# A hybrid decoder layer on one core: weight splits moved behind each slot's steps, deeper buffers for the last pair's output weights, an earlier load of the first pair's q

## The chip, the cores and the metric

One core of one Trainium2 chip. The metric is the device time of one execution in microseconds (us), median of several runs; lower is better. Short names: PE is TensorE, PEld its weight loads, DVE is VectorE, ACT is ScalarE, POOL is GpSimd, SP is SyncE, which here only issues DMAs.

## What is computed

One layer over 1024 tokens of width 2048, in float32 (the reference cut to what matters):

```
h = rms_norm(x); proj = h @ w_in                       # 2048 x 7448
A: 12 heads of 64, dilated causal windows (128,1),(512,4),(2048,16), QK norm, mixed by softmax denominators
B: 8 heads of 64, causal softmax attention with a forget bias c[t]-c[s], QK norm
C: 4 heads of gated linear attention (dk 96, dv 192), per-head RMS norm
mixed = concat(out_a * silu(az), out_b * silu(bz), out_c * silu(cz))
out = x + mixed @ w_out                                # 2048 x 2048
```

## The kernel before, in words

**Precision.** Each wide product is done as three matmuls on rounded halves: a float32 matrix is split into hi (ACT copies it, rounding) and lo (DVE subtracts hi from the raw values), and hi·hi, hi·lo and lo·hi are summed. The activations (act_hi, act_lo) are split once and stay in SBUF. The weights are streamed: a quarter is 128 x 512 numbers (256 KB); SP loads it into w_raw (2 places), ACT writes w_hi (`split_hi`, L827), DVE writes w_lo (`split_lo`, L1231), PE uses both. A split of a place waits until PE is done with the quarter that was there, and a load until the raw place has been split.

**Groups and slots.** The input projection goes in 58 groups of 128 columns. A group has four quarters, each used for two halves of the tokens, so 8 half quarters of 12 matmuls. Everything else is cut into steps and laid between them: a group has 8 slots, and in a slot PE does the slot's steps and then one half quarter (`group` of each engine, L877, L1234, L1708). In slots 0, 2, 4 and 6, ACT and DVE split the quarter after the next one and then do their steps of the slot. ACT evicts the results and stores them in DRAM (proj), from where the heads load them.

**GLA heads (C).** Four heads of three groups, 24 slots (`gla_steps`, numbers of slots at L77). Slot 1: gate. Slot 3: DVE's scan of the decay (L1373). From slot 6 on, seven levels, one per slot: DVE takes differences (L1384, L1385), ACT the exponential (L993), POOL makes q_level and k_level (L776, L779), two slots later PE multiplies them (L1782) and DVE puts the result under a mask (L1436). Slot 12 transposes v, slot 18 is the chain of seven states on DVE (L1410, L1413), slot 19 the silu of z (DVE L1421, then three wide activations on ACT), slot 20 the output (ACT L1023, L1029), slot 21 its norm on DVE (L1424), slot 23 the transposes on PE (L1827) and the final product.

**Attention pairs (A and B).** Ten pairs of heads, 32 slots each. A pair has 16 items (head, block of 128 queries); an item's score (L1874), mask (L1514) and exponential (L1105), scaling (L1524), transposes (L1887), split of the transposed weights (pt_hi L1113, pt_lo L1530) and product with v (L1901) stand in fixed slots (`steps_of`, L109). Between them stand the norms of the next pair's q and k: ACT squares (L1062), DVE sq_lo (L1458), PE sums (L1847), ACT log and root, DVE the norm, and in slot 26 and slot 2 of the next pair the stacks: ACT q_st and k_hi (L1082, L1083), DVE a cast to the other half (L1473), POOL the low parts (L801, L804). For the first pair these stand in one group of their own before it (`first_steps_of`): squares in slots 1, 2, 4, 5.

**Last pair.** Its first 8 slots carry the last group of the projection; the other 24 carry early quarters of the output projection (45 quarters of w_out, three rounds over 3, 3 and 2 tiles of tokens), at the slots of EARLY_SLOT: nine quarters in five slots. Their sums with the residual (`early_sums`, L1627) go to DRAM as partial. The rows of mixed are loaded and split meanwhile (`mix_hi_part` L1205, `mix_lo_part` L1633, slots 4 to 13). Their landing, and that of the weights (L582), is ordered by SP's program, which is in order: mixed and weights interleaved, the load of the last gate behind quarter 6 and a wait for eleven mix_lo parts, the residuals behind quarter 7, partial stores and their reloads three quarters into a round. Then follow three groups of 16 output quarters over all 8 banks (`out_quarter`, L1967).

**What sets the order.** Each engine and SP's queue run their own program strictly in order; semaphores between them count finished work. A wait in one step holds up all that stands behind it on that engine.

```
def group(s, row, steps):            # ACT, before
    for slot in range(8):
        if slot % 2 == 0:
            split_hi(s, slot // 2 + 1)
        ...
        steps(slot)
```

Of the kernel before, what the change touches and what calls it, by code (L numbers as in the profile page):

```python
# [15 lines left out]
P = 128  # L16
SEQ = 1024
# [81 lines left out]
EARLY = len(ROUNDS) * (KT - 1)  # L99
EARLY_SLOT = [8 + (n * 5) // 9 for n in range(EARLY)]  # L100
# [73 lines left out]
def build(nc, x, norm_g, w_in, a_q_gain, a_k_gain, b_q_gain, b_k_gain, fox_bias,  # L174
# [11 lines left out]
    with ExitStack() as ctx:  # L186
# [65 lines left out]
        gla = ExitStack()  # L252
        level_mask = sb("level_mask", [P, LEVELS, HEAD], scope=gla)
# [9 lines left out]
        ranks = ExitStack()  # L263
        rank_rows = sb("rank_rows", [GATE_ROWS, SEQ], F32R, scope=ranks)
        ranks.close()
        v_rows = sb("v_rows", [P, NT, C_DV], scope=gla)
        k_rows = sb("k_rows", [P, NT, C_DK], scope=gla)
        state = sb("state", [C_DK, NT, C_DV], scope=gla)
# [9 lines left out]

        pairs = ExitStack()
# [29 lines left out]

        def mix_row(k):  # L310

            return vz[:] if k in (LAST - 1, LAST) else act_lo[:, k, :].bitcast(F32)

# [55 lines left out]
        w_in_sem = [sem("w_landed0"), sem("w_landed1")]  # L369
        x_in = [sem(f"x_landed{b}") for b in range(X_BUFS)]  # L370
# [10 lines left out]
        def _(sp):  # L381
# [196 lines left out]
            def load_out_rows(n, kk, col):  # L578

                sp.wait_ge(lo_done, Q_OUT + n - 1)  # L580
                slot = (EARLY + kk) % 2 if not isinstance(n, int) else n % 2
# [12 lines left out]
            load_k(0, 0, A_WIDTH, 0)  # L594
# [57 lines left out]
            for n in range(2, EARLY):  # L652
                load_out_rows(n, n % (KT - 1), 0)
# [164 lines left out]
        def _(act):  # L818
# [20 lines left out]
            def split_hi_out(cg, kk):  # L839

                slot = (EARLY + kk) % 2
# [8 lines left out]
                act.wait_ge(w_in_sem[slot], 16 * (2 * (GROUPS + AHEAD) + (KT // 2) * (cg - 1) + (EARLY + kk) // 2 + 1))  # L850
                act.activation(w_hi[:, slot, :], w_raw[:, slot, :], ACT.Copy).then_inc(hi_done, 1)  # L851

            def split_hi_early(n):

                r, kk = (n - 2) // (KT - 1), (n - 2) % (KT - 1)
# [1165 lines left out]
```

## Time and profile before

| | us |
|---|---|
| median of 3 runs | 2213.92 |
| lowest, highest | 2213.67, 2214.6 |
| the profiled execution | 2212.89 |
| its span, first to last instruction | 2211.1 |
| mean granted clock of PE, share of full speed | 0.991 |

The profile is of one execution. Its views used below: the page (busy time of each engine, its share of the span, number of instructions); waits (engine and line, the engine and line it waited for, us in total, times, longest); windows (start and end, length, busy us and instructions of each engine, PEclk as share of full speed, DMA share, GB/s); timelines (start us, duration us, engine, line, operation, output<-inputs, shape, count, and in brackets the idle time before it and what ended it).

### The profile page before, as it was taken

What the parts mean: (1) busy time and instruction counts of PE and PEld (TensorE: products, weight loads), DVE (VectorE), ACT (ScalarE), POOL (GpSimd) and SP (SyncE); (2) the same over time, 40 slices, a digit from 0 to 9 for tenths busy, and PEclk for the clock granted to TensorE, in tenths of its full rate; (3) what the DMA queues carried; (4) which work ended last, traced back from release to release, by engine and by line L of the source; (5) the groups of instructions that cost most, each with busy time, mean ns of one, the idle gap of its engine ahead of it and who ended that gap; (6) DMA issues with size and microseconds to landing.
All of it is one profiled execution on the core that took longest, in us unless ns stands there. A gap on an engine that the chain in (4) does not pass through costs nothing.

```text
span 2211.1 us, 30018 instructions
## 1 busy us (share of the span) xinstructions
PE 2141.1 (97%) x11016; PEld 1815.6 (82%) x11016; DVE 972.3 (44%) x1611; ACT 865.4 (39%) x1466; POOL 239.9 (11%) x141
## 2 busy tenths in 40 slices
PE   6999999999989999999999999999999989899999
PEld 5788888888878888888888888888888867778887
DVE  6611436445434545444444445444444455522122
ACT  7311343434444444454444444454444454311110
POOL 0000324142320000001010000001010000000000
PEclk9999999999999999999999999999999999999999
DMA  6323323333132222222222222322222253323134
GB/s 217 78 67 86 94 69 91 102 76 104 49 103 70 63 76 72 85 67 66 72 71 81 71 70 76 94 81 79 64 90 81 84 207 118 119 100 106 69 126 143
DMA packets 189772, 201.16 MB, mean 91 GB/s; under 512 B 15992, under 2 KB 138920, under 8 KB 188544
## 3 DMA queue, kind: packets, MB, share of 16 engines
q1 hardware_dynamic: 172976, 169.70, 26.2%
q10 hardware_dynamic: 16720, 30.45, 3.7%
q8 instruction: 47, 0.77, 0.1%
q14 instruction: 29, 0.24, 0.0%
HBM read 151.33 MB, written 48.78 MB: 91 GB/s over the span
## 4 chain that ended last, share of the span: by engine, by line
PE 86%; DVE 4%; ACT 3%; issue 3%; DMA 3%; POOL 1%; ACTq 0%; SPq 0%; DVEq 0%; POOLq 0%
PE acc L1694 18%; PE acc L1696 18%; PE acc L1695 18%; PE turned L1887 3%; PE pv L1902 3%; PE pv L1901 3%; PE scores L1877 2%; DMA w_raw<-in_w_out_dram 2%; PE scores L1874 2%; PE pv L1782 1%; PE acc L1984 1%; PE turned L1984 1%; PE scores L1984 1%; PE turned L1985 1%; PE scores L1985 1%
## 5 line engine op out<-in xcount | busy, mean ns | idle before, releaser
L1694 PE MATMUL acc<-act_hi,w_hi 128*128 128x512 f32 x1856 | 740.9, 399 | 7.0 <-DVE w_lo L1231 2.4
L1696 PE MATMUL acc<-act_hi,w_lo 128*128 128x512 f32 x1856 | 727.4, 392 | 0.0
L1695 PE MATMUL acc<-act_lo,w_hi 128*128 128x512 f32 x1856 | 725.9, 391 | 0.0
L1231 DVE TENSOR_TENSOR w_lo<-w_raw,w_hi 128x512 fp32r<-128x512 f32 x224 | 182.3, 814 | 578.8 <-ACT w_hi L827 578.5
L1694 PEld LDWEIGHTS acc<-act_hi,w_hi 128*128 128x128 f32 x1856 | 350.8, 189 | 78.2 <-DVE w_lo L1231 5.0
L1696 PEld LDWEIGHTS acc<-act_hi,w_lo 128*128 128x128 f32 x1856 | 350.0, 189 | 76.8
L1695 PEld LDWEIGHTS acc<-act_lo,w_hi 128*128 128x128 f32 x1856 | 350.9, 189 | 67.1
L827 ACT ACTIVATE w_hi<-w_raw 128x512 fp32r<-128x512 f32 x224 | 140.8, 628 | 294.8 <-PE acc L1696 249.6
L1105 ACT ACTIVATE prob<-prob,neg_max 128x128 f32<-128x128 f32 (+7 forms) x160 | 124.5, 778 | 274.1 <-DVE neg_max L1514 274.1
L1530 DVE TENSOR_TENSOR pt_lo<-turned,pt_hi 128x128 fp32r<-128x128 f32 (+7 forms) x160 | 121.0, 756 | 160.6 <-ACT pt_hi L1113 159.7
L801 POOL TENSOR_TENSOR q_st<-raw,q_st 64x1024 fp32r<-64x1024 f32 x20 | 55.8, 2788 | 1053.2 <-ACT q_st L1082 1053.2
L1902 PE MATMUL pv<-pt_lo,v_st 128*128 128x128 f32 x720 | 169.1, 274 | 0.0
L1901 PE MATMUL pv<-pt_hi,v_st 128*128 128x128 f32 x720 | 160.8, 264 | 0.9 <-DVE pt_lo L1530 0.9
L1113 ACT ACTIVATE pt_hi<-turned 128x128 fp32r<-128x128 f32 (+7 forms) x160 | 103.5, 647 | 130.6 <-PE turned L1887 128.3
L1901 PEld LDWEIGHTS pv<-pt_hi,v_st 128*128 128x128 f32 x720 | 137.7, 191 | 7.6 <-DVE pt_lo L1530 1.3
L1902 PEld LDWEIGHTS pv<-pt_lo,v_st 128*128 128x128 f32 x720 | 137.7, 191 | 6.0
L1658 DVE TENSOR_TENSOR w_lo<-w_raw,w_hi 128x512 fp32r<-128x512 f32 x48 | 33.3, 693 | 213.3 <-ACT w_hi L851 213.3
L869 ACT ACTIVATE stage<-acc 128x512 f32<-128x512 f32 x112 | 66.8, 597 | 149.2 <-PE acc L1696 149.1
L851 ACT ACTIVATE w_hi<-w_raw 128x512 fp32r<-128x512 f32 x49 | 31.0, 632 | 229.1 <-PE side L1986 215.0
L1514 DVE CUSTOM_DVE_ANT_0 prob<-scores,logit_bias 128x128 f32<-128x128 f32 (+7 forms) x160 | 120.0, 750 | 0.5
L1887 PE MATMUL turned<-ident,prob 128*128 128x128 f32 x720 | 108.7, 278 | 2.5 <-DVE prob L1524 2.5
L1874 PE MATMUL scores<-k_hi,q_st 128*128 128x512 f32 (+1 forms) x240 | 90.4, 377 | 2.0 <-issue 1.2
(273 smaller groups left out, 2777.7 us busy)
## 6 DMA issues: line engine op xcount, KB each, us to landing
w_raw<-in_w_in_dram SPq DMA_DIRECT2D x240, 256.0 KB, 2.9
proj_scratch<-stage ACTq DMA_DIRECT2D x116, 256.0 KB, 2.1
w_raw<-in_w_out_dram SPq DMA_DIRECT2D x94, 256.0 KB, 3.1
raw<-proj_scratch SPq DMA_DIRECT2D x20, 512.0 KB, 3.5
act_lo<-mixed_scratch SPq DMA_DIRECT2D x7, 1024.0 KB, 5.1
res<-in_x_dram SPq DMA_DIRECT2D x24, 256.0 KB, 5.6
out_dram<-res SPq DMA_DIRECT2D x24, 256.0 KB, 3.1
sq<-proj_scratch SPq DMA_DIRECT2D x10, 512.0 KB, 3.4
```

The source lines that it names most:

```text
L827: act.activation(w_hi[:, slot, :], w_raw[:, slot, :], ACT.Copy).then_inc(hi_done, 1)
L1105: act.activation(prob[:, j % 2, 0:n], prob[:, j % 2, 0:n], ACT.Exp, scale=-1.0, bias=neg_max[:, j:j + 1], accum_out=denom[:, j:j + 1]).the ...
L1231: dve.tensor_tensor(w_lo[:, slot, :], w_raw[:, slot, :], w_hi[:, slot, :].bitcast(F32), ALU.subtract)\
L1514: dve.tensor_tensor_reduce(out=prob[:, j % 2, 0:n], in0=scores[:, 0:n], in1=bias, scale=1.0, scalar=3e38, op0=ALU.add, op1=ALU.min, accum_ ...
L1530: dve.tensor_tensor(pt_lo[:, 0:n], turned[:, 0:n], pt_hi[:, 0:n].bitcast(F32), ALU.subtract)\
L1694: pe.matmul(acc, hi, xh, start=first, stop=False)
L1695: pe.matmul(acc, hi, xl, start=False, stop=False)
L1696: mm = pe.matmul(acc, lo, xh, start=False, stop=end)
L1874: pe.matmul(scores[:, c0:c1], q, k_hi[:, h, c0:c1], start=True, stop=False)
L1887: mm = pe.transpose(turned[:, at], prob[:, j % 2, at], ident[:])
L1901: pe.matmul(o, v_st[:, h, t, :], pt_hi[:, at], start=(t == 0), stop=False)
L1902: mm = pe.matmul(o, v_st[:, h, t, :], pt_lo[:, at], start=False, stop=(t == i))
```

## The change

1. In `group` of ACT and DVE the split of a quarter comes behind the slot's steps; in the GLA heads slot 20 (G_OUT) keeps it ahead. In the last group of the projection the fourth split is that of early quarter 0, and early quarter 1 is split behind the group.
2. Early quarters get four places to land (two new ones, extra_raw, beside w_raw) and three for splits (extra_hi, extra_lo); they are split two ahead, behind the steps of the slot, and the sums of a round come ahead of the slot's steps. The new places lie in the memory of raw, so SP waits for the last pair's stacks before the first load, and the first four are loaded before mixed rows 4 to 6.
3. The output stage starts with tiles 2 to 7, then 0 and 1, each waiting only for the sums that its bank needs. Quarter and place are counted from the stage's start.
4. q of the first pair is loaded at the end of the last GLA head, once all level matmuls are done and the older group with its columns is stored, ahead of two weight quarters and of the head's store; k before the wait for that store. For this the GLA tiles are laid out anew: k_level lies where raw will, q_level where sq will.

```
+        k_level = sb("k_level", [C_DK, 2, SEQ], scope=gla)
+        q_level = sb("q_level", [C_DK, 2, HALF], scope=gla)
+        g_b = sb("g_b", [C_DK, SEQ], scope=gla)
...
+        v_rows = sb("v_rows", [P, NT, C_DV], scope=gla)
+        k_rows = sb("k_rows", [P, NT, C_DK], scope=gla)
+        state = sb("state", [C_DK, NT, C_DV], scope=gla)
         level_mask = sb("level_mask", [P, LEVELS, HEAD], scope=gla)
...
         g_z = sb("g_z", [C_DK, 2, SEQ], scope=gla)
-        g_b = sb("g_b", [C_DK, SEQ], scope=gla)
         g_t = sb("g_t", [C_DK, 2, SEQ], scope=gla)
-        q_level = sb("q_level", [C_DK, 2, HALF], scope=gla)
-        k_level = sb("k_level", [C_DK, 2, SEQ], scope=gla)
...
+        extra_raw = sb("extra_raw", [P, 2, HALF], scope=extra)
+        extra_hi = sb("extra_hi", [P, HALF], F32R, scope=extra)
+        extra_lo = sb("extra_lo", [P, HALF], F32R, scope=extra)
...
+        early_raws = [extra_raw[:, 0, :], w_raw[:, 0, :], extra_raw[:, 1, :], w_raw[:, 1, :]]
+        early_his = [w_hi[:, 0, :], extra_hi[:], w_hi[:, 1, :]]
+        early_los = [w_lo[:, 0, :], extra_lo[:], w_lo[:, 1, :]]
...
 def saved_of(pair, g):
     if first_pair(pair):
-        saved(S_FIRST_V if g == 2 else S_FIRST_V - 1)
+        saved(S_FIRST_V - (HEAD_GROUPS + 1, 1, 0)[g])
...
+def load_early_rows(n):
+    if n >= EARLY_RAWS:
+        sp.wait_ge(lo_done, Q_OUT + n - EARLY_RAWS + 1)
+    elif n % 2 == 1:
+        sp.wait_ge(lo_done, Q_OUT + n // 2 - 1)
+    sp.dma_start(early_raws[n % EARLY_RAWS], w_out_k[:, OUT_ORDER[n % (KT - 1)], 0:HALF])\
+        .then_inc(early_landed(n)[0], 16)
...
+sp.wait_ge(gla_lv, LEVELS * C_HEADS)
+load_q(0, 0, 0)
 for kq in range(2):
     load_quarter(S_FIRST_V, kq, 2 * A_WIDTH)
 store_head(C_HEADS - 1)
-load_q(0, 0, 0)
-
+load_k(0, 0, A_WIDTH, 0)
 sp.wait_ge(gla_saved, 16 * C_HEADS)
-load_k(0, 0, A_WIDTH, 0)
...
 load_mixed(0)
 load_mixed(1)
-load_out_rows(0, 0, 0)
+for split in (ql_done, qh_done, kh_done, k_other_done, kl_done):
+    sp.wait_ge(split, 2 * PAIRS)
+load_early_rows(0)
+load_early_rows(1)
 load_mixed(2)
 load_mixed(3)
-load_out_rows(1, 1, 0)
+load_early_rows(2)
+load_early_rows(3)
 load_mixed(4)
...
-def group(s, row, steps):
+def group(s, row, steps, first=None, split_after=None):
     for slot in range(8):
-        if slot % 2 == 0:
+        if slot == first:
             split_hi(s, slot // 2 + 1)
         if slot == 7:
             evac(s, 0)
         steps(slot)
+        if slot % 2 == 0 and slot != first:
+            (split_after or split_hi)(s, slot // 2 + 1)
     evac(s, 1)
     save(s, row)
...
+                group(S_LAST_Z, COL_B + 3 * B_WIDTH + (B_PAIRS - 1) * P, steps, split_after=split_last)
+                split_hi_early(1)
                 for slot in range(8, SLOTS + 1):
+                    steps(slot)
+                    for n in early_at(slot):
+                        split_next(n + 2)
...
+                for slot in range(8, SLOTS + 1):
+                    for n in early_at(slot):
+                        if n % (KT - 1) == 0 and n > 0:
+                            early_sums(n // (KT - 1) - 1)
+                    steps(slot)
+                    for n in early_at(slot):
+                        if n + 2 < EARLY:
+                            split_lo_early(n + 2)
+                        elif n + 2 == EARLY:
+                            split_lo_group(1, 0)
...
+                for t in (2, 3, 4, 5, 6, 7, 0, 1) if first else range(NT):
+                    if first and t == 6:
                         pe.wait_ge(o_summed, 4 * PAIRS)
-                        pe.wait_ge(partial_summed, NT)
+                    elif first and t in (7, 0, 1):
+                        pe.wait_ge(partial_summed, {7: ROUNDS[1][-1], 0: ROUNDS[2][0], 1: ROUNDS[2][1]}[t] + 1)
```

DVE's `group` changes in the same way as ACT's.

## Rows read from the trace of the kernel before

**Rows 1.** The page: busy us, share of the span and instructions.

```profile
PE 2141.1 (97%) x11016; PEld 1815.6 (82%) x11016; DVE 972.3 (44%) x1611; ACT 865.4 (39%) x1466; POOL 239.9 (11%) x141
```

**Rows 2.** Waits of PE over the span: us in total, times, longest.

```profile
PE acc L1944 <- DVE w_lo L1619: 17.5, 11, 3.6
...
PE side L1847 <- DVE sq_lo L1458: 8.8, 10, 4.9
PE pv L1782 <- POOL k_level L779: 6.1, 4, 1.6
...
PE turned L1887 <- DVE prob L1524: 2.5, 1, 2.5
PE acc L1984 <- DVE sq L1627: 2.5, 1, 2.5
...
PE acc L1944 <- DVE sq L1627: 0.8, 1, 0.8
```

**Rows 3.** Windows around and behind PE's gaps; the clock stands third from the end.

```profile
256.00:268.00 12.00, 10.44 (x56) 8.78 (x55) 9.37 (x9) 4.59 (x6) 9.50 (x6) 0.86 0.50 133
350.00:362.00 12.00, 10.52 (x63) 9.03 (x62) 9.90 (x10) 4.78 (x6) 8.34 (x6) 1.00 0.56 153
444.00:458.00 14.00, 12.45 (x58) 10.56 (x56) 9.92 (x10) 5.83 (x7) 9.75 (x6) 0.76 0.54 131
541.00:554.00 13.00, 11.44 (x60) 9.65 (x59) 10.43 (x10) 5.04 (x7) 8.93 (x6) 0.87 0.55 141
...
626.50:631.00 4.50, 4.50 (x13) 3.49 (x12) 1.39 (x2) 1.95 (x4) 0.00 (x0) 0.59 0.24 60
...
1790.00:1850.00 60.00, 47.49 (x220) 38.95 (x220) 36.66 (x51) 28.54 (x41) 0.00 (x0) 0.89 0.39 132
```

**Rows 4.** Timeline of the fourth GLA head, slot 6: weight subtract, first level.

```profile
539.69 0.69 DVE L1231 TENSOR_TENSOR w_lo<-w_raw,w_hi 128x512 fp32r<-128x512 f32 x1 [2.27 <-ACT w_hi L827]
540.30 0.68 DVE L1384 TENSOR_TENSOR g_t<-g_b 96x512 f32<-96x512 f32 x1
...
544.27 1.49 POOL L779 TENSOR_TENSOR k_level<-g_qk,g_t 96x512 f32<-96x512 f32 x1
```

**Rows 5.** Timeline at the end of the second and fourth GLA heads.

```profile
415.26 1.76 DVE L1424 TENSOR_TENSOR g_qk<-g_qk,o_rstd 128x1536 f32<-128x1536 f32 x1 [0.73 <-ACT o_rstd L1034]
...
417.45 1.04 PE L1827 MATMUL scores<-ident,g_qk 128*96 128x128 f32 x8
...
608.68 1.76 DVE L1424 TENSOR_TENSOR g_qk<-g_qk,o_rstd 128x1536 f32<-128x1536 f32 x1 [1.12 <-ACT o_rstd L1034]
...
610.58 1.05 PE L1827 MATMUL scores<-ident,g_qk 128*96 128x128 f32 x8
```

**Rows 6.** Timeline of ACT in the group before the first pair: its first square.

```profile
623.57 0.63 ACT L1062 ACTIVATE sq<-raw 128x512 f32<-128x512 f32 x1 [5.41 <-DMA raw<-proj_scratch]
```

**Rows 7.** Timeline of PE in the last pair: five of its eleven waits for w_lo.

```profile
1803.40 0.50 PE L1944 MATMUL acc<-w_hi,act_hi 128*128 128x512 f32 x1 [2.22 <-DVE w_lo L1619]
...
1841.93 0.79 PE L1944 MATMUL acc<-w_hi,act_hi 128*128 128x512 f32 x1 [2.31 <-DVE w_lo L1619]
...
1866.85 0.50 PE L1944 MATMUL acc<-w_hi,act_hi 128*128 128x512 f32 x1 [0.53 <-DVE w_lo L1619]
...
1907.24 0.50 PE L1944 MATMUL acc<-w_hi,act_hi 128*128 128x512 f32 x1 [1.29 <-DVE w_lo L1619]
...
1930.41 0.50 PE L1944 MATMUL acc<-w_hi,act_hi 128*128 128x512 f32 x1 [1.42 <-DVE w_lo L1619]
```

**Rows 8.** Timeline: a DVE operation beside one of POOL, in a head and in slot 26.

```profile
602.85 4.70 DVE L1231 TENSOR_TENSOR w_lo<-w_raw,w_hi 128x512 fp32r<-128x512 f32 x1 [6.39 <-ACT w_hi L827]
...
870.54 2.65 POOL L801 TENSOR_TENSOR q_st<-raw,q_st 64x1024 fp32r<-64x1024 f32 x1 [85.37 <-ACT q_st L1082]
871.00 2.75 DVE L1473 CAST k_hi<-raw 64x1024 fp32r<-64x1024 f32 x1
...
876.42 0.39 PE L1874 MATMUL scores<-k_hi,q_st 128*128 128x512 f32 x1
```

More of the change, by code:

```diff
@@ L99 @@
 EARLY = len(ROUNDS) * (KT - 1)
+EARLY_RAWS, EARLY_SPLITS = 4, 3
 EARLY_SLOT = [8 + (n * 5) // 9 for n in range(EARLY)]
@@ L651, in _ @@
             load_mixed(6)
-            for n in range(2, EARLY):
-                load_out_rows(n, n % (KT - 1), 0)
+            for n in range(4, EARLY):
+                load_early_rows(n)
                 if n == 6:
@@ L839, in split_hi_out @@
             def split_hi_out(cg, kk):
-                slot = (EARLY + kk) % 2
+                slot = kk % 2
                 if kk == 1:
@@ L1038, in gla_head @@
                 for g in range(HEAD_GROUPS):
-                    group(C_ALONE + HEAD_GROUPS * c + g, col[g], lambda slot: gla_steps(c, 8 * g + slot))
+                    group(C_ALONE + HEAD_GROUPS * c + g, col[g], lambda slot: gla_steps(c, 8 * g + slot),
+                          G_OUT - 8 * g)
             gla_head(0)
@@ L1174, in steps, with split_last @@
                             mix_hi_part(kk)
-                group(S_LAST_Z, COL_B + 3 * B_WIDTH + (B_PAIRS - 1) * P, steps)
-                for slot in range(8, SLOTS + 1):
-                    last_pair_slot(slot, lambda: steps(slot))
-            def last_pair_slot(slot, steps):
-                ahead = [n + 1 for n in early_at(slot)]
-                for n in ahead[:1]:
-                    split_next(n)
-                steps()
-                for n in ahead[1:]:
-                    split_next(n)
+                def split_last(s, kq):
+                    if kq < 4:
+                        split_hi(s, kq)
+                    else:
+                        split_hi_early(0)
+                group(S_LAST_Z, COL_B + 3 * B_WIDTH + (B_PAIRS - 1) * P, steps, split_after=split_last)
+                split_hi_early(1)
+                for slot in range(8, SLOTS + 1):
+                    steps(slot)
+                    for n in early_at(slot):
+                        split_next(n + 2)
             def split_next(n):
@@ L1232, in split_lo, with group @@
                     .then_inc(lo_done, 1)
-            def group(s, steps):
+            def group(s, steps, first=None, split_after=None):
                 for slot in range(8):
-                    if slot % 2 == 0:
+                    if slot == first:
                         split_lo(s, slot // 2 + 1)
                     steps(slot)
+                    if slot % 2 == 0 and slot != first:
+                        (split_after or split_lo)(s, slot // 2 + 1)
             def split_lo_half(n, kq):
@@ L1448, in gla_head @@
                 for g in range(HEAD_GROUPS):
-                    group(C_ALONE + HEAD_GROUPS * c + g, lambda slot: gla_steps(c, 8 * g + slot))
+                    group(C_ALONE + HEAD_GROUPS * c + g, lambda slot: gla_steps(c, 8 * g + slot), G_OUT - 8 * g)
             gla_head(0)
@@ L1652, in add_residual @@
                     dve.tensor_tensor(to, banks[t], to, ALU.add).then_inc(out_summed, 1)
-            def split_lo_group(cg, kk):
-                slot = (EARLY + kk) % 2
-                dve.wait_ge(hi_done, Q_OUT + EARLY + KT * (cg - 1) + kk + 1)
-                dve.tensor_tensor(w_lo[:, slot, :], w_raw[:, slot, :], w_hi[:, slot, :].bitcast(F32),
-                                  ALU.subtract).then_inc(lo_done, 1)
             for kk in range(KT):
@@ L1969, in out_quarter @@
                 at_end = kk == KT - 1
-                slot = EARLY % 2 if only else (EARLY + kk) % 2
+                slot = 0 if only else kk % 2
                 k = OUT_ORDER[kk]
@@ L1974, in out_quarter @@
                     pe.wait_ge(mix_lo, KT)
-                for t in range(NT):
-                    if kk == 0 and isinstance(cg, int):
+                first = kk == 0 and isinstance(cg, int)
+                for t in (2, 3, 4, 5, 6, 7, 0, 1) if first else range(NT):
+                    if first and t == 6:
                         pe.wait_ge(o_summed, 4 * PAIRS)
-                        pe.wait_ge(partial_summed, NT)
-                    elif kk == 0 or only:
+                    elif first and t in (7, 0, 1):
+                        pe.wait_ge(partial_summed, {7: ROUNDS[1][-1], 0: ROUNDS[2][0], 1: ROUNDS[2][1]}[t] + 1)
+                    elif not first and (kk == 0 or only):
                         pe.wait_ge(out_summed, NT * (cg - 2) + t + 1)
```

70 lines of the change are left out of this document (37 added, 33 removed).

## The prediction

> **What bounds the kernel now.** I read the page's shares first: TensorE is busy 97% of the span [rows 1], VectorE 44%. What the change can win is therefore TensorE's idle time, 70 us, and what a low clock costs after it. Next I asked for TensorE's waits, longest first in total [rows 2]. Four of those groups lie where the diff works: 17.5 us on the low parts of output weights (L1944), 8.8 us on sq_lo (L1847), 6.1 us on k_level (L1782), and 2.5 us each on prob (L1887) and on the partial sums (L1984). The waits of the start, before 110 us, are not touched. Then I read windows around the gaps for the granted clock [rows 3], and the timelines of all engines for what each gap hung on. The sum is made against the profiled execution, 2212.89 us with a span of 2211.1; the median shown, 2213.92, is 1.0 above it, and I add 1.0 at the end.
>
> **Split behind the steps, in general.** Nothing is added or removed here: one ScalarE copy and one VectorE subtract per weight quarter change places with the steps of their slot. TensorE needs the pair of them two half quarters later, and a half quarter of 12 matmuls takes some 2.7 us at full clock (4.5 us at clock 0.59 [rows 3]). So the split may be up to 5.4 us late, plus TensorE's own steps. In an attention slot the steps end with mask, exponential and perhaps a stack, some 4 us behind TensorE's score; the copy and subtract cost 0.6 to 0.7 each. I went through each even slot of the pair this way and found no deadline missed, with some 2.3 us left in the tightest, slot 26. The weight loads on SP wait for the subtract of two quarters before, so they go out later by the same 1 to 5 us, but are also wanted later; what stands behind them on SP (gate, values, next q and k) is released by stores that land later still. Cost 0, cover 2.3 us.
>
> **GLA levels, four heads.** TensorE's first level matmul (slot 8) waits 1.5 us for GpSimd's k_level, four times [rows 2]. The chain behind it: VectorE's slot 6 subtract of weights at 539.69, only then the decay differences at 540.30, an exponential, GpSimd until 545.76 [rows 4]. Before that subtract VectorE had stood idle 2.27 us for ScalarE's copy, which waits for TensorE. With the differences ahead of the subtract the chain starts 2.27 + 0.61 = 2.9 us earlier (the memset of slot 2, moved ahead of its subtract, adds a little), and the wait goes whole: 6.1. After three of the four waits the clock is low: 0.86 of 12 us, 0.76 of 14 and 0.87 of 13, which is 1.7, 3.4 and 1.7 lost; after one of them it stays at 1.00 [rows 3]. So the clock is worth 0 to 6.8 and I take 6.8, as the low stretch directly follows the gap each time. Gain 12.9.
>
> **End of a GLA head.** Here the new order costs. In slot 18 VectorE now subtracts weights after the seven state steps and before slot 19's maximum of g_z, on which ScalarE's chain (three wide activations, the output copies and squares) hangs. That chain ends in VectorE's normalisation, and TensorE's transposes wait for it: in the fourth head it ends at 610.44 and they start at 610.58. In the second head there are 0.43 us between [rows 5]. The chain is 0.6 later: 0.6 in two heads, 0.3 in the two with such slack. Loss 1.8, bounds 0 and 2.4.
>
> **First pair's q.** In the group before the first pair TensorE waits 4.9 us in one place [rows 2]: ScalarE's square had waited 5.4 us for the load of raw [rows 6], issued behind the store of the previous group. The diff waits for an older group and issues it in the last head, into memory that the level matmuls have left. Then squares and subtract end about 0.5 us before TensorE wants them. The 4.5 us after the gap ran at clock 0.59 [rows 3]: another 1.8. Of the 6.7, something comes back: k takes q's old place in the DMA queue, the third weight quarter lands behind it (before, too, ScalarE waited for it), and ScalarE, waiting for it in order, holds up the second log. I charge 0.5, bounds 0 and 3. The next wait, of the first score on GpSimd's stacks, hangs on TensorE's own sums and stays. Gain 6.2.
>
> **Nine pairs, slot 17.** The remaining nine waits on sq_lo make 8.8 − 4.9 = 3.9. Each is 0.4 to 0.5; mask, exponential and square stood behind the split in slot 16 (0.6 and 0.7), more than the wait. Gain 3.9.
>
> **Last pair.** Four landing places, three split places, and two quarters of lookahead. But both kernels split a slot's first quarter at the same point: behind the steps of the slot before. What goes is what hung on a second quarter, on landing or on a freed place: 0.5, 1.3 and 1.4 [rows 7], and the 2.5 of the partial sums, since the output stage now starts on four banks that hold none [rows 2]. What stays: 2.3 at 1841.93 [rows 7], behind an exponential, a mix copy and a mix subtract; the longest, 3.6 [rows 2], since the load of the eighth quarter still stands on SP behind the wait for mix_lo and the gate load; the 2.5 on prob, where the split moved from before to after and VectorE has as much ahead of it; some 0.8 for a round's sums, as now [rows 2]. At 1803.40 [rows 7] the landing is early now, but the steps of slot 8 (a gated product and a mix subtract of 1.2 each) hold the split: 2.2 becomes 0.9. The extra early loads stand in front of three mixed loads, which are not yet due. Gain 5.7 + 1.3 = 7.0; bounds: −3, if the loads delay the mixes, and the whole, below.
>
> **Sum.** 12.9 − 1.8 + 6.2 + 3.9 + 7.0 = 28.2. 2212.89 − 28.2 + 1.0 = 2185.7 us, 1.3% faster.
>
> **Rivals.**
> *Last pair nearly dense.* If the deeper places hide my remaining waits too, the last pair gives its 23.3 us of waits (17.5 + 2.5 + 2.5 + 0.8 [rows 2]) and 6.6 of slow clock (0.89 of 60 us [rows 3]), less 4.1 for sums and prob: 25.8 in place of 7.0, 2166.9 us. For it: TensorE's need per slot is above the others' busy time. Against: the chain of one slot is a latency, not a load.
> *Low clock stays.* If short matmuls in the GLA slots, not the gap, bring the clock down, levels give 6.1, the first group 4.4, the last pair 4: 6.1 − 1.8 + 4.4 + 3.9 + 4 = 16.6, 2197.3 us. For it: one 1.5 us gap without a fall.
> *The delay shows.* A new wait of 0.6 us on w_lo in each of the 50 groups from the first GLA head on would cancel it all, 2213 us. Against it the 2.3 us of cover.
> *A blocked subtract, slower.* Place: slot 26 of nine pairs. GpSimd's q low part starts at 870.54 and VectorE's cast after it takes 2.75; a weight subtract beside GpSimd's wide multiply of a head took 4.70 in place of 0.69 [rows 4, 8]. In the new order the cast should start at 869.8 and GpSimd at 870.0. If the cast loses, it ends at 873.2 and the weight subtract behind it waits for the next GpSimd op too, to 876; pt_lo and the mask follow, and TensorE's score at 876.42 [rows 8] comes 2.0 late. With 1.7 of slow clock each, 9 × 3.7 = 33 us: 2219 us. It decides from 28.2/9 = 3.1 us per pair. Against it: 0.2 us of lead, and a clock that need not fall. The Trainium skill (SBUF — State Buffer, Who interferes with whom) has a rule that speaks for this rival: a VectorE instruction with two SBUF inputs and a GpSimd one that reads SBUF shut each other out for a whole instruction, and the first to start wins. By that rule the weight subtract, now among the stacks, is always exposed and the cast's lead settles it; the 4.70 us row agrees.
>
> **How the numbers follow.** Forecast 0.53; low clock stays 0.22; last pair dense 0.12; delay shows 0.06; blocked subtract 0.07. Faster by over 0.2% (4.4 us, about what a measurement of this kernel can tell): 0.53 + 0.22 + 0.12 = 0.87; within it 0.06; slower 0.07. The range reaches 16 us beyond the forecast to the slow side, past the low-clock case, and 15 to the fast side, most of the way to the dense one: 2171 to 2202.
>
> **What would show it.** Right: no wait on k_level and clock 1.00 behind slot 8 of each head; TensorE's wait on g_qk (L1424's row) up to about 2 us in total; sq_lo waits under 1 us in total; no wait of the first output quarter on sums; 3 to 4 us still lost at the eighth early quarter. Wrong: waits on w_lo (L1231's row) above 3 us, casts of 2.75 followed by subtracts over 2 us in slot 26, or a score waiting for neg_max in every pair.

## The result, and the profile after

| | before | after |
|---|---|---|
| median, us | 2213.8 (4 runs) | 2177.01 (4 runs) |
| lowest, highest | 2212.33, 2214.6 | 2176.43, 2179.62 |
| the profiled execution | 2212.89 | 2176.6 |
| its span | 2211.1 | 2174.9 |

The ratio is 0.9837, with a 95% interval of 0.9825 to 0.9849: 36.8 us less. Forecast were 28.2 us less, 2185.7, with a range of 2171 to 2202. So direction and range held, and the gain was a quarter under-estimated. The question is which terms of the sum were short.

The page of the changed kernel, as for [rows 1]:

```profile
PE 2129.0 (98%) x11016; PEld 1807.6 (83%) x11016; DVE 1000.6 (46%) x1611; ACT 859.6 (40%) x1466; POOL 248.6 (11%) x141
```

TensorE has the same instructions and is busy 12.1 us less: some 9 of that is clock, an estimate from the mean granted clock of the two traces, 0.991 and 0.995. The rest of the gain is idle time. VectorE became 28 us busier with as many instructions, so some of its work is slower now. The page's group of its weight subtracts shows where, 207.6 us in place of 182.3:

```profile
L1266 DVE TENSOR_TENSOR w_lo<-w_raw,w_hi 128x512 fp32r<-128x512 f32 x223 | 207.6, 931 | 300.7 <-ACT w_hi L857 300.7
```

That costs nothing as long as nothing waits for it.

Waits of TensorE in the changed kernel, as in [rows 2] (total, times, longest, in us):

```profile
PE acc L1981 <- DVE w_lo L1656: 7.8, 6, 2.2
...
PE acc L1981 <- DVE extra_lo L1656: 3.1, 1, 3.1
PE acc L1731 <- DVE w_lo L1266: 3.0, 8, 1.4
PE turned L1924 <- DVE prob L1561: 2.5, 1, 2.5
...
PE acc L1981 <- DVE stage L1671: 0.5, 1, 0.5
PE scores L1864 <- DVE g_qk L1461: 0.2, 1, 0.2
```

The group on k_level is gone, and those on sq_lo and on the output sums; the 17.5 us on the early quarters' low parts are 7.8 + 3.1. The 2.5 us on prob are still there.

To see where the gain came from (36.7 us between the two traces up to the last matmul; the spans differ by 36.2), I took the first start of some TensorE instructions in both timelines and subtracted. The last column is what each stage gained.

```
stage, from the first start of ... to ...             before    after   gained
start of the program to head 1's gate matmul                              0.4
four heads, gate matmul to first level matmul                             6.8   (1.70, 1.66, 1.66, 1.76)
four heads, first level matmul to last transposes                         4.8   (1.35, -0.47, 2.78, 1.14)
last head's transposes to first pair's values         656.17   637.28     6.9
nine pairs                                                                6.0   (0.59 to 0.72 each)
last pair, values to first early quarter             1796.28  1769.35     2.1
first to last early quarter                          1935.95  1901.96     7.1
to the first output quarter                          1939.30  1902.65     2.7
output                                                                    0.1
```

(The columns give the time of the stage's end mark.) The clock behind slot 8 of a head, windows of the changed kernel at the places of [rows 3] (the granted clock third from the end):

```profile
256.00:268.00 12.00, 12.00 (x79) 10.82 (x78) 10.70 (x10) 4.30 (x5) 9.00 (x5) 1.00 0.46 132
...
442.00:456.00 14.00, 14.00 (x88) 12.21 (x86) 12.50 (x12) 5.13 (x7) 11.80 (x7) 1.00 0.41 112
535.00:548.00 13.00, 13.00 (x82) 11.35 (x81) 12.12 (x11) 4.56 (x7) 10.83 (x6) 1.00 0.44 121
```

TensorE is busy for every microsecond of them and keeps its upper level, where it had 0.86, 0.76 and 0.87. The last pair still has its gaps, in TensorE's timeline:

```profile
1776.02 0.50 PE L1981 MATMUL acc<-w_hi,act_hi 128*128 128x512 f32 x1 [0.74 <-DVE w_lo L1656]
...
1789.43 0.51 PE L1981 MATMUL acc<-w_hi,act_hi 128*128 128x512 f32 x1 [1.76 <-DVE w_lo L1656]
1796.23 0.50 PE L1981 MATMUL acc<-extra_hi,act_hi 128*128 128x512 f32 x1 [3.06 <-DVE extra_lo L1656]
...
1813.81 0.73 PE L1981 MATMUL acc<-w_hi,act_hi 128*128 128x512 f32 x1 [2.24 <-DVE w_lo L1656]
```

The first answers to the 2.22 at 1803.40 in [rows 7] (0.9 was forecast), the last to the 2.31 at 1841.93, the third to the 3.6 that was forecast to stay.

### The profile page after: what moved, and what is told of

The parts are those of the page before. It is cut to its first block, busy times and chain, and to the rows that moved or that the text cites. A ratio compares the mean times of both kernels' runs of the same rounds, so it can differ in the third digit from the quotient of the medians.

```text
span 2174.9 us, 30011 instructions
## 1 busy us (share of the span) xinstructions
PE 2129.0 (98%) x11016; PEld 1807.6 (83%) x11016; DVE 1000.6 (46%) x1611; ACT 859.6 (40%) x1466; POOL 248.6 (11%) x141
## 4 chain that ended last, share of the span: by engine, by line
PE 88%; DVE 5%; ACT 3%; DMA 2%; issue 2%; SPq 0%; ACTq 0%; DVEq 0%
PE acc L1731 18%; PE acc L1733 18%; PE acc L1732 18%; PE turned L1924 4%; PE pv L1939 4%; PE pv L1938 3%; PE scores L1914 2%; PE scores L1911 2%; PE pv L1819 1%; DMA w_raw<-in_w_in_dram 1%; PE side L1819 1%; PE turned L2023 1%; PE scores L2023 1%; PE acc L2023 1%; PE scores L2024 1%
## 5 line engine op out<-in xcount | busy, mean ns | idle before, releaser
L1266 DVE TENSOR_TENSOR w_lo<-w_raw,w_hi 128x512 fp32r<-128x512 f32 x223 | 207.6, 931 | 300.7 <-ACT w_hi L857 300.7
L1663 DVE TENSOR_TENSOR w_lo<-w_raw,w_hi 128x512 fp32r<-128x512 f32 x49 | 33.9, 693 | 214.5 <-ACT w_hi L881 214.5
```

Source lines behind the costliest of these rows:

```text
L1266: dve.tensor_tensor(w_lo[:, slot, :], w_raw[:, slot, :], w_hi[:, slot, :].bitcast(F32), ALU.subtract)\
```

## The experiments

Each kernel is the changed one with one edit, and each was timed in five rounds beside the kernel before. Where a difference is small, I go by the stage marks of its trace against those of the changed kernel, since medians of one kernel differ by a microsecond or two between sets of runs. One stage is too unsteady for that. From the first to the last early quarter the changed kernel took 132.6 us, and the traces of e1 to e5, e7, e9 and e10, which leave the order of that work alone, took 129.7 to 135.0. A difference there counts only if a named gap or an earlier mark stands outside the same nine traces.

**e1. One split back ahead, in the GLA heads.** (`first` takes a list of slots, on ScalarE and VectorE.)

```diff
-    group(C_ALONE + HEAD_GROUPS * c + g, ..., G_OUT - 8 * g)
+    group(C_ALONE + HEAD_GROUPS * c + g, ..., [G_OUT - 8 * g, G_LEVEL[0] - 8 * g])
```

> The changed kernel with one weight split, that of slot 6 of each GLA head, put back ahead of the slot's steps on ScalarE and VectorE. Theory: this split alone is what the k_level wait hung on, and the low clock behind it hangs on that gap: TensorE waits about 1.5 us on k_level in each of the four heads (6.1 in all), the clock falls behind at least three of them, and the time is 11 to 14 us above the changed kernel's 2177.0, that is 2188 to 2191. Rival, low clock from the short matmuls of those slots: the wait returns but nothing on top of it, +6 us, 2183. Rival, the whole group's splits matter and not this one: within 2 us of 2177.

Measured: 2191.88 us (2189.49 to 2193.51), ratio 0.9902 (0.9884 to 0.9921). Its wait on k_level, and the windows behind slot 8 of its four heads:

```profile
PE pv L1819 <- POOL k_level L809: 6.1, 4, 1.6
```

```profile
259.00:273.00 14.00, 13.85 (x85) 12.09 (x85) 12.90 (x10) 3.91 (x5) 9.73 (x8) 1.00 0.37 100
353.00:367.00 14.00, 13.73 (x70) 12.12 (x70) 12.53 (x9) 2.64 (x4) 9.38 (x7) 0.76 0.35 104
451.00:465.00 14.00, 14.00 (x80) 12.27 (x80) 12.66 (x11) 4.22 (x5) 9.93 (x7) 0.88 0.34 93
547.00:561.00 14.00, 14.00 (x79) 12.29 (x80) 12.76 (x10) 4.16 (x5) 9.92 (x7) 0.88 0.34 99
```

From the gate of head 1 to the end of head 4 it lost 13.1 us: 6.8 up to the level matmuls and 6.3 between them and the heads' ends. So one split decides the whole item. It also settles the rival on the clock: the same short matmuls run at 1.00 without the gap and at 0.76 and 0.88 with it, in three of four heads (before, it was another three: head 2 was spared there, head 1 here). A gap of 1.5 us costs 3.3 us a head on average: 2.0 in the head that was spared, 3.2 to 4.7 in the others.

**e2. One split back ahead, in the nine pairs.**

```diff
-    group(s0 + g, columns[g], lambda slot, g=g: steps_at(pair, 8 * g + slot))
+    group(s0 + g, columns[g], lambda slot, g=g: steps_at(pair, 8 * g + slot), [16 - 8 * g])
```

> The changed kernel with one weight split of each of the nine full pairs, that of slot 16, put back ahead of the steps on both engines. Theory: the nine waits on sq_lo hung on it alone. They come back at 0.4 to 0.5 us each, and since each pair became 0.59 to 0.72 shorter and not 0.43, the time is 5 to 7 us above 2177.0, 2182 to 2184. Rival: the pairs gained by the delay of all their splits together; then this one split gives back 0 to 2 us, 2177 to 2179.

Measured: 2184.63 us (2182.83 to 2185.48), ratio 0.9870 (0.9850 to 0.9891). Its waits of TensorE on sq_lo:

```profile
PE side L1884 <- DVE sq_lo L1495: 4.2, 10, 0.5
```

The pairs are 0.59 to 0.73 us longer each, 5.9 us in all, which is what the change had gained there. Nine waits of some 0.43 us stand for stages 0.66 us longer: the idle time in a row is less than what the stage loses. In the first pair, the last product's matmul and the sum behind it start at 693.16 and 693.84, 0.68 us apart; the same two start 0.11 apart in the changed kernel. That is 0.57 us lost, where the row has 0.41 in brackets.

**e3. The first pair's q loaded late.**

```diff
-            load_q(0, 0, 0)
             for kq in range(2):
                 load_quarter(S_FIRST_V, kq, 2 * A_WIDTH)
             store_head(C_HEADS - 1)
+            load_q(0, 0, 0)
             load_k(0, 0, A_WIDTH, 0)
```

> The changed kernel with the first pair's q loaded behind the store of the last head and behind two weight quarters, as before the change. Theory: the first group's gain of 6.9 us was this load alone: one wait of 4 to 5 us on g_qk (L1461's row) returns with low clock behind it, 2182.5 to 2184.5. Rival: the splits behind the steps gave part of it, as they let the first square start earlier; then at most 4 us return, below 2181.

Measured: 2180.90 us (2180.36 to 2182.52), ratio 0.9855 (0.9834 to 0.9876), which by the time alone is the rival's range, just below 2181. Up to the first pair's values it lost 4.3 us of the 6.9 gained: 3.1 up to the first sum and 1.2 behind it, where the clock was 0.89 from 616 to 620 us and 1.00 in the changed kernel. But this run undid only the load's place. The change did a second thing to it: it waits for the rows of an older group. ScalarE's first square, which in the kernel before had stood idle 5.4 us [rows 6]:

```profile
610.40 0.63 ACT L1097 ACTIVATE sq<-raw 128x512 f32<-128x512 f32 x1 [2.56 <-DMA raw<-proj_scratch]
```

It waits for the load here too, but only 2.6 us. The load was issued 0.5 us behind the head's store here (603.49, the store at 602.97), and 6.0 us behind it before (620.16, the store at 614.17). Counted from the last head's transposes, the square starts 11.0 us later here and 13.0 before. So the place is worth 4.3 us of the 6.9. The other 2.6 were not tried alone; the square's 2 us point to the group waited for. The load itself took longer here, 6.9 us to land beside the store and 3.4 before, so most of the earlier issue was not gained. The rival's reason, that the splits gave part of it, isn't needed: in both kernels the square waited last for the load. TensorE's wait is on sq_lo (2.9 us) and not on g_qk, as I had written in the expectation by a slip.

**e4. The output's first quarter in plain order.**

```diff
-                for t in (2, 3, 4, 5, 6, 7, 0, 1) if first else range(NT):
+                for t in range(NT):
```

(and both waits ahead of the first tile)

> The changed kernel with the first output quarter's eight row tiles in plain order, the waits for the output sums and the last partial sums all ahead of the first tile. Theory: 2.5 us of wait return there, 2179.5. Rival: the sums are done early enough now, since the last round's split no longer stands behind them; then under 0.5 us, 2177 to 2177.5.

Measured: 2180.51 us (2179.59 to 2182.94), ratio 0.9854 (0.9833 to 0.9875). The wait is back in TensorE's timeline:

```profile
1906.08 0.47 PE L2022 MATMUL acc<-w_hi,act_hi 128*128 128x512 f32 x1 [2.18 <-DVE sq L1671]
```

The last early matmul starts at 1903.05, 3.0 us ahead of this one; in the changed kernel it is 0.7. That part gives 2.3 us, as forecast.

**e5 and e9. The blocked subtract.** In the changed kernel VectorE's k cast in slot 26 starts 0.14 us before GpSimd's q low part and takes 0.69 us, in all nine pairs; before it had started behind it and taken 2.75 [rows 8]. So the race that the rival hung on was there, and the cast won it. (The twenty casts take 13.8 us in all, 32.3 before.) I delayed the cast:

```diff
                     elif name == "stack0" and next_kind is not None:
-                        stack(pair + 1, 0)
+                        [dve.memset(spare[:, 44 * i:44 * i + 44], 0.0) for i in range(3)]; stack(pair + 1, 0)
```

> The changed kernel with three small memsets (44 columns each, some 0.3 us together) ahead of VectorE's k cast in slot 26 of each of nine pairs, so that the cast starts after GpSimd's q low part instead of 0.14 us before it. The rival of the prediction, blocked subtract: the cast takes about 2.75 us, the weight subtract behind it is late or waits for GpSimd's next multiply, TensorE's next score or weight quarter comes late by 2 us, with low clock 3.7: up to 33 us above 2177.0, 2210. My theory: the cast does lose and takes 2.75, but the cover of 2.3 us takes most of it; 0 to 0.7 us per pair, 2177 to 2183. If the cast still takes 0.69, the race was not lost and nothing is said on it.

Measured: 2176.82 us (2175.89 to 2179.33), ratio 0.9838 (0.9820 to 0.9856). GpSimd and VectorE in slot 26 of the third pair:

```profile
851.09 2.91 POOL L831 TENSOR_TENSOR q_st<-raw,q_st 64x1024 fp32r<-64x1024 f32 x1 [85.61 <-ACT q_st L1117]
```

```profile
850.87 0.20 DVE L1609 MEMSET spare<- 128x44 f32 x3
851.08 0.69 DVE L1510 CAST k_hi<-raw 64x1024 fp32r<-64x1024 f32 x1
```

The three memsets took 0.20 us together, too little: the cast was at most 0.01 us ahead in all nine pairs, and that was enough. Nothing is said on the rival. So again, with a longer delay:

```diff
-                        [dve.memset(spare[:, 44 * i:44 * i + 44], 0.0) for i in range(3)]; stack(pair + 1, 0)
+                        [dve.reciprocal(spare[:, i:i + 1], eps_col[:]) for i in range(4)]; stack(pair + 1, 0)
```

> The changed kernel with four reciprocals of one column (some 0.2 us each) ahead of VectorE's k cast in slot 26 of nine pairs: the memsets of the earlier run moved the cast by only 0.15 us, it started 0.01 us before GpSimd's q low part and still took 0.69 us. Now it should start some 0.5 us behind GpSimd. Blocked subtract, as the prediction priced it: the cast takes about 2.3 us (until GpSimd's op ends), the weight subtract behind it starts 3 us late or more, and TensorE loses 2.0 us or with low clock 3.7 per pair: 2195 to 2210. My theory: the cast loses, but TensorE waits at most 0.7 us per pair for it, as the weight quarter is due 2.3 us later: 2177 to 2183.

Measured: 2188.61 us (2188.05 to 2190.12), ratio 0.9892 (0.9877 to 0.9907). The same slot, GpSimd, then VectorE, then TensorE's score:

```profile
851.72 2.40 POOL L831 TENSOR_TENSOR q_st<-raw,q_st 64x1024 fp32r<-64x1024 f32 x1 [85.61 <-ACT q_st L1117]
854.19 2.73 POOL L834 TENSOR_TENSOR k_lo<-raw,k_hi 64x1024 fp32r<-64x1024 f32 x1
```

```profile
851.46 0.34 DVE L1609 RECIPROCAL spare<-eps_col 128x1 f32<-128x1 f32 x4
851.81 2.85 DVE L1510 CAST k_hi<-raw 64x1024 fp32r<-64x1024 f32 x1
854.69 2.78 DVE L1266 TENSOR_TENSOR w_lo<-w_raw,w_hi 128x512 fp32r<-128x512 f32 x1
857.40 0.94 DVE L1567 TENSOR_TENSOR pt_lo<-turned,pt_hi 128x768 fp32r<-128x768 f32 x1
```

```profile
859.40 0.50 PE L1911 MATMUL scores<-k_hi,q_st 128*128 128x512 f32 x1 [0.84 <-DVE neg_max L1551]
```

The cast starts 0.09 us behind GpSimd and takes until GpSimd has ended; the weight subtract behind it falls into GpSimd's second operation and takes 2.78; pt_lo and the mask are late behind both, and the score waits. This is the chain that the prediction named, link by link. Its price was wrong: each pair is 0.9 to 1.1 us longer, 9.5 in all, not 3.7 each. My own theory was wrong as well: the time lies between its range, which ended at 2183, and the rival's, which began at 2195. (The median is 11.6 us above the changed kernel's; the other 2 us lie in the early quarters.) The wait is 0.8 and not 2.0 us, and the clock stays at 1.00 over the windows of these pairs. By the rule that the prediction took from the Trainium skill (SBUF — State Buffer, Who interferes with whom), whoever starts first shuts the other out for a whole instruction; the rows agree, with the cast at 0.69 when it leads by 0.01 us and at 2.85 when it trails by 0.09.

**e6. The eighth early quarter's load first.**

```diff
                 load_early_rows(n)
-                if n == 6:
+                if n == 7:
                     sp.wait_ge(mix_lo, KK_GATED + 1)
                     load_gate(LAST, last_column)
```

> The changed kernel with SP's load of the eighth early quarter ahead of its wait for the mixed low part and the gate load, one queue place earlier. Theory: the longest wait of the last pair (3.06 us, on extra_lo, behind that late load) goes down to what a 2 us load issued some 8 us earlier leaves, under 0.7, and the 1 to 2 us of low clock behind it go too: 3 to 5 us below 2177.0, 2172 to 2174. Rival: the split itself is held by the steps of its slot (an exponential, a mix copy and subtract) and the load was not what it hung on last; under 1 us, 2176 to 2177.

Measured: 2173.38 us (2173.18 to 2178.03), ratio 0.9832 (0.9812 to 0.9851). The load goes out at 1776.85 and no longer at 1789.18, and the gap of 3.06 us at the eighth quarter is gone. But the ninth has one now:

```profile
1799.06 0.50 PE L1981 MATMUL acc<-w_hi,act_hi 128*128 128x512 f32 x1 [1.60 <-DVE w_lo L1656]
```

Its load stands where the eighth's was, behind the gate load and four residual loads. From the first to the last early quarter the kernel is 3.2 us shorter, but its waits there are only 1.4 us shorter, and the rest is clock. At the 2.24 us gap behind them it stands 41.3 us behind the first early quarter, and the nine traces with the old order of loads stand at 43.1 to 46.0: at least 1.8 us come from the edit. The times alone don't show it, as they overlap those of the changed kernel.

**e7. Slot 18's split back ahead of the state steps, in the heads.**

```diff
-    group(C_ALONE + HEAD_GROUPS * c + g, ..., G_OUT - 8 * g)
+    group(C_ALONE + HEAD_GROUPS * c + g, ..., [G_OUT - 8 * g, G_STATE - 8 * g])
```

> The changed kernel with the split of slot 18 of each GLA head put back ahead of the state steps (slot 20 is already so). Theory: this is the subtract that lies 0.6 us in the chain at a head's end, of which 0.47 us per head reached TensorE; four heads give 1.9 us, 2175.1. Rival: the state steps, now 0.7 us later, hold back TensorE's use of the state or the maximum behind them as much as the subtract did: 2177 or up to 3 us above.

Measured: 2175.20 us (2173.78 to 2177.91), ratio 0.9833 (0.9815 to 0.9852). Each head is 0.33 to 0.37 us shorter behind its level matmuls, 1.4 in all, of the 0.47 that the new order cost there. Part of it goes by a way that I had not listed: four waits of 0.18 us on w_lo, new in the changed kernel, are gone too. That w_lo is slot 20's subtract, which runs until GpSimd's wide multiply ends (in head 4 they take 4.69 and 4.62 us), and the multiply hangs on the same chain from slot 19's maximum.

**e8. The early quarters' loads in their old places on SP.**

```diff
             load_early_rows(0)
-            load_early_rows(1)
             load_mixed(2)
             load_mixed(3)
-            load_early_rows(2)
-            load_early_rows(3)
+            load_early_rows(1)
             load_mixed(4)
             load_mixed(5)
             load_mixed(6)
-            for n in range(4, EARLY):
+            for n in range(2, EARLY):
```

> The changed kernel with SP issuing the first early quarters of output weights in the places of before: the second behind the fourth mixed load, the third and fourth behind all seven. The four landing places and three split places stay. Theory: the last pair's gain of 11.8 us has the earlier loads for a part only; what needs them are the first two or three waits, 2 to 4 us with the clock behind them: 2179 to 2181. Rival: the deeper split lookahead alone did it and the loads land in time anyway: within 1 us of 2177. Rival: the early loads are the whole, 10 us or more, 2187.

Measured: 2181.37 us (2179.63 to 2182.65), ratio 0.9859 (0.9837 to 0.9881). The first gap of the early quarters, 0.74 us in the changed kernel, is

```profile
1778.81 0.80 PE L1981 MATMUL acc<-w_hi,act_hi 128*128 128x512 f32 x1 [4.26 <-DVE w_lo L1656]
```

From first to last early quarter it lost 4.1 us, and its median is 4.55 above that of e5, timed in the same rounds, with no overlap. The first gap ends 8.62 us behind the first early quarter, where it was 6.67 in the changed kernel and 7.12 before: with the new lookahead and the loads in their old places it ends later than before the change, not earlier. At this gap it is the places that pay.

**e10. The last pair's full group with splits ahead.**

```diff
-                group(S_LAST_Z, ..., steps, split_after=split_last)
+                group(S_LAST_Z, ..., steps, (0, 2, 4, 6), split_after=split_last)
```

> The changed kernel with the four splits of the last pair's one full group (slots 0, 2, 4 and 6, the last of them the first early quarter) put back ahead of the steps on both engines. Theory: these gave 1.5 to 2.7 us of the last pair's 11.8 (the wait of 0.9 on pt_lo in slot 6, and the 2.05 gained up to the first early quarter): 2178.5 to 2179.7. Rival: all of that came from the early loads, which no longer stand behind a split; under 0.5 us, 2177.0 to 2177.5.

Measured: 2178.62 us (2176.04 to 2180.30), ratio 0.9848 (0.9835 to 0.9862). In its timeline the wait that I had overlooked is back:

```profile
1759.19 0.33 PE L1938 MATMUL pv<-pt_hi,v_st 128*128 128x128 f32 x1 [0.89 <-DVE pt_lo L1567]
```

and the first early quarter starts 1.8 us later. Only the wait, 0.9, is the edit's for certain: e1 and e5, with the changed kernel's splits here, start it 1.1 us later too, by a lower clock. The median is within the changed kernel's range. Behind the first early quarter this execution gained 2.9 us on the one of the changed kernel, with the same gaps within 0.9 us: there the clock was kinder. The windows of the changed kernel and of e10, over the same work within 2 us:

```profile
1805.00:1825.00 20.00, 17.76 (x89) 14.76 (x89) 10.85 (x15) 7.71 (x12) 0.00 (x0) 0.91 0.20 67
```

```profile
1805.00:1825.00 20.00, 17.74 (x100) 15.09 (x99) 12.49 (x17) 8.64 (x13) 0.00 (x0) 1.00 0.25 81
```

**e11 and e12. Putting together what helped.** e11 is e6 and e7 with one edit more: from slot 8 of the last pair the mixed rows' copies and subtracts go behind the slot's early splits.

> Three edits on the changed kernel: the eighth early quarter's load ahead of the wait for the mixed low part (alone it gave 3.2 us at that place), slot 18's split ahead of the state steps (alone 1.4 us at the heads' ends), and new, from slot 8 of the last pair the mixed rows' copies and subtracts behind the slot's early splits, since the mixes are due one to three slots later. Theory: the gaps of 1.76 and 2.24 us on w_lo at two early quarters become 0 and about 1.1, with some low clock 2.5 to 4 us: 2177.0 less 3.2, 1.5 and 3.2 is 2169. Rival: the mixes become late in their place and TensorE waits for the mixed low part instead; then 2172 or above.

Measured: 2172.27 us (2170.32 to 2172.80), ratio 0.9816 (0.9803 to 0.9830). The gaps of 0.74 and 1.76 are gone (the first is absent in e1 and e5 too, so it says nothing), but in their place stands

```profile
1798.42 0.80 PE L1993 MATMUL acc<-w_hi,act_hi 128*128 128x512 f32 x1 [6.00 <-DVE w_lo L1668]
```

This was not the rival as written: the mixes are in time. The ninth quarter's load, issued at 1791.17 behind the gate and the residuals, landed only then; ScalarE's copy of it:

```profile
1797.01 0.63 ACT L895 ACTIVATE w_hi<-extra_raw 128x512 fp32r<-128x512 f32 x1 [5.23 <-DMA extra_raw<-in_w_out_dram]
```

TensorE, freed of its earlier gaps, came to it sooner. The time is 3 us above the theory's 2169. e12 moves those five loads too, and two copies of slot 6 into ScalarE's idle time (the diff is against e11):

```diff
-                if n == 7:
+                if n == 9:
                     sp.wait_ge(mix_lo, KK_GATED + 1)
                     load_gate(LAST, last_column)
-                if n == 7:
+                if n == 11:
                     sp.wait_ge(silu_done, LAST)
```

> The combination before with two more edits. The gate load and the four residual loads move on SP from behind the seventh and eighth early quarter's load to behind the tenth and twelfth, so that the ninth and tenth no longer land behind them (that was a wait of 6.0 us, where two waits of 1.6 and 2.3 on VectorE had been before). And ScalarE's two mixed copies of slot 6 come ahead of that slot's exponential, in the 2.0 us in which it idles. Theory: the 6.0 us go down to under 1, the wait of 2.5 us on prob to about 0.9, with 1 to 2 us of low clock: 2172.3 less 7 to 9 is 2163 to 2165. Rival: the gate or the sums come late behind and TensorE waits for them instead; then 2170 or above.

Measured: 2165.29 us (2163.94 to 2165.56), ratio 0.9783 (0.9770 to 0.9796): 11.7 us below the changed kernel and 47.6 below the one before. The gaps that are left around these places, and the window over the last pair:

```profile
1765.25 0.63 PE L1938 MATMUL turned<-ident,prob 128*128 128x128 f32 x4 [0.56 <-DVE prob L1569]
...
1791.48 0.50 PE L1995 MATMUL acc<-w_hi,act_hi 128*128 128x512 f32 x1 [1.14 <-DVE w_lo L1670]
```

```profile
1735.00:1910.00 175.00, 165.98 (x854) 138.36 (x854) 103.80 (x173) 82.87 (x135) 5.13 (x2) 1.00 0.50 169
```

No gap there is over 1.2 us up to 1814 (one of 2.10 stays at 1860.76), and the clock is 1.00 over the 175 us, where it was 0.96 in the changed kernel.

## Why the prediction was right, and where it was short

The gain was 8.6 us above the forecast: 0.5 in the heads, 0.7 at the first pair, 2.1 in the nine pairs, 4.8 in the last pair, and 0.5 before and behind, where nothing was forecast.

*Split behind the steps, in general: cost 0.* Right in the pairs, where no wait on w_lo is new. In the heads four of 0.18 us are, 0.7 us together, which brings the waits on w_lo to 3.0 us, the very bound that was to show the forecast wrong. VectorE's weight subtracts took 25 us longer in total (42 of them over 1 us, 19 before), where they now fall beside GpSimd's work. The cover hid nearly all of that; the forecast had named the exposure in its last rival and put no size on it.

*GLA levels, four heads: 12.9, and end of a GLA head: −1.8.* Together 11.1, measured 11.6. e1 ties the gap and the clock to one split, with 13.1. Taken apart, the levels gave 13.5 and the ends cost 1.9, if head 2's 0.47 stands for all four. That 0.47 us was measured in head 2, the one head whose clock was full in both traces, and e7 gives back 1.4 for four by moving one split: the charge of 1.8 was of the right size.

*First pair's q: 6.2.* Measured 6.9. The 0.5 charged for the third quarter's landing did not show, and that is most of the difference. The working named the group waited for and the place without sizing either; e3 gives 4.3 to the place.

*Nine pairs, slot 17: 3.9.* Measured 6.0: mis-sized. The step added the idle times of the rows, 0.4 to 0.5 each. e2 brings back rows of that size and 5.9 us. The difference is not clock (1.00 over all pairs, before and after, and 1.00 in e2 in the 4.5 us from the wait on): how long TensorE's row stands idle is modelled from the ends of matmuls, and the stage marks, which need no ends, say 0.66.

*Last pair: 7.0.* Measured 11.8, the largest miss. Of the terms that were named, 0.5, 1.3 and 2.5 us are gone and 1.42 became 0.25. What stays did stay: 2.24, 3.06, 2.50 on prob.

One term came in by luck: 2.22 at 1803.40 became 0.74, where 0.9 was forecast. TensorE's clock was 0.74 between the first early quarter and the end of that gap, so TensorE came late to it. In e4 it was 1.00, and the same wait is longer than before the change:

```profile
1777.62 0.50 PE L1981 MATMUL acc<-w_hi,act_hi 128*128 128x512 f32 x1 [2.31 <-DVE w_lo L1656]
```

e2 and e9 have 2.31 too. The wait ends 6.67 us behind the first early quarter in the changed kernel and in e4 alike, and ended 7.12 behind it before. So this item brought 0.45 us and not 1.3.

The step that fell short is the list of what goes. It took from the eleven waits on w_lo those shown in [rows 7], and passed over two more, and one on pt_lo, a wait of the split in slot 6 itself, whose return e10 shows. In the trace of before:

```profile
1783.67 0.33 PE L1901 MATMUL pv<-pt_hi,v_st 128*128 128x128 f32 x1 [0.90 <-DVE pt_lo L1530]
...
1861.44 0.50 PE L1944 MATMUL acc<-w_hi,act_hi 128*128 128x512 f32 x1 [0.71 <-DVE w_lo L1619]
...
1870.38 0.50 PE L1944 MATMUL acc<-w_hi,act_hi 128*128 128x512 f32 x1 [0.74 <-DVE w_lo L1619]
```

These, with 0.5 of the 3.6, 0.3 of the sums' 0.8 and 0.1 on neg_max, are 3.3 us; summed up, the idle rows account for 10.4, and 1.4 us are clock and modelled ends. Of that, 1.1 us is luck too: it is the clock behind the 2.5 us wait on prob, and in e1 and e5 that stretch is 1.1 us longer again.

e8, e4 and e10 size the parts that can be undone alone: loads 4.1, output order 2.3, the full group's splits 0.9 by their wait. The rest, some 4.5 us (three split places, deeper lookahead, and clock), was not tried alone, and the parts need not add up.

*The rivals.* Last pair nearly dense: not here, but e12 comes close to it (23.6 us by the marks, with its clock at 1.00) by other places for loads on SP and for the mixed rows' copies and subtracts; whether the argument against it, that a slot's chain is a latency, holds for what e12 has left (2.10 us on w_lo at 1860.76 and gaps below 1.2) was not tried. Low clock stays: refuted by e1. The delay shows: only in the four waits of 0.18 us. Blocked subtract: true in its mechanism, decided by a lead of 0.14 us where 0.2 was forecast, and priced three and a half times too high; with it the change would have gained some 27 us in place of 36.8, still faster.

## What to carry to other kernels

When gaps are summed for a forecast, list every one with its releaser before deciding which go, and where a stage repeats, size it from marks at its ends and not from the idle time in brackets. Where a queue issues loads in program order, a wait for something not yet due (a mixed row, residual rows) is paid by the load behind it, and curing one load moves the price to the next until the waits themselves stand later. A VectorE operation that beats GpSimd by some hundredths of a microsecond is worth a note in the code: 0.1 us the other way cost 9.5 us here. And before a difference between two traces is put down to an edit, look how far the same stage moves between traces in which it was not touched.

## What the runs showed of the hardware that I had not expected

A lead of 0.01 us decided a race between VectorE and GpSimd (0.69 us against 2.85 for the same cast). It was no chance of one run: e5 has it in nine pairs, and in the kernel before ten casts of the other stack (slot 2) start 0.01 to 0.02 us ahead, take 0.69, and GpSimd's operation beside them takes 2.94 to 2.96. The stakes are not even. GpSimd's first operation takes 2.40 us where it wins (e9) and 2.91 where it loses (e5): it waits out the rest of a short cast. VectorE waits out GpSimd's operation, finishes its cast in the change-over (854.12 to 854.66 in e9), and its next instruction meets GpSimd's next one: 2.85 and 2.78 us back to back.

The clock does not follow a gap every time. With the same four gaps of 1.5 us in the heads it fell in three, but head 2 was spared in one kernel and head 1 in another. Behind the last pair's gaps the 20 us from 35.7 us behind the first early quarter ran at 0.91 in four of the nine traces with one order of that work, the changed kernel, e1, e3 and e5, and at 1.00 in the other five. In the same nine the stage from first to last early quarter took 129.7 to 135.0 us, more than several of the edits measured here gave. A lower clock also hides a wait: the first gap of that stage is 2.31 us at clock 1.00, 0.74 at 0.74, and none at 0.67 (e1), with the matmul behind it starting within 0.8 us of the same place each time. The gaps of 0.6 to 0.8 us in the pairs (e9) never brought the clock down.
